# A two-block network on one core: the column halves of block two's norms cross the stage borders separately

## What is computed

```python
def rms_norm(x, g):
    xf = x.astype(jnp.float32)
    y = xf * lax.rsqrt(jnp.mean(xf * xf, axis=-1, keepdims=True) + EPS)
    return (y * g.astype(jnp.float32)).astype(x.dtype)

def ada_norm(h, g, shift, scale):
    return rms_norm(h, g) * (1 + scale) + shift

def second_block(...):
    h, hc = x, ctx
    for l in range(DEPTH):
        ...
        h = h + HALF * gt1 * swiglu(ada_norm(h, g_ffn1[l], sh1, sc1), w1_ffn1[l], w3_ffn1[l], w2_ffn1[l])
        hc = hc + HALF * cgt1 * swiglu(ada_norm(hc, g_ffn1[l], csh1, csc1), w1_ffn1[l], w3_ffn1[l], w2_ffn1[l])

        u = ada_norm(h, g_mix[l], sh2, sc2)
        uc = ada_norm(hc, g_mix[l], csh2, csc2)
        z_conv, z_cq, z_ckv, z_kr, z_four = split_mixing(u @ w_in[l])
        zc_conv, zc_cq, zc_ckv, zc_kr, zc_four = split_mixing(uc @ w_in[l])
        ...
        h = h + gt2 * y
        if not last:
            ...
            hc = hc + cgt2 * yc

        h = h + HALF * gt3 * swiglu(ada_norm(h, g_ffn2[l], sh3, sc3), w1_ffn2[l], w3_ffn2[l], w2_ffn2[l])
        if not last:
            hc = hc + HALF * cgt3 * swiglu(ada_norm(hc, g_ffn2[l], csh3, csc3), ...)
    return rms_norm(h, g_final)
```

## Time and profile before

| | us |
|---|---|
| median of 3 runs | 2830.51 |
| lowest, highest | 2826.48, 2833.05 |
| the profiled execution | 2829.12 |
| its span, first to last instruction | 2827.3 |
| busy in the span: PE / DVE / ACT / POOL | 2741.4 / 1776.6 / 1065.5 / 192.0 |

### The profile page before, as it was taken

How to read it: one execution, slowest core, us unless ns; L and a number is a source line. 1 busy time by engine, 2 the same in 40 slices (tenths; PEclk the granted TensorE clock), 3 DMA queues, 4 the chain that set the end, 5 groups by cost and what they waited for, 6 DMA issues and landing times.

```text
span 2827.3 us, 45215 instructions
## 1 busy us (share of the span) xinstructions
PE 2741.4 (97%) x16508; PEld 2334.7 (83%) x16508; DVE 1776.6 (63%) x3023; ACT 1065.5 (38%) x1704; POOL 192.0 (7%) x184
## 2 busy tenths in 40 slices
PE   8999999999999999999999999999999999899998
PEld 8669999589988888775777788888788888689998
DVE  7466656566676565587675665555665557756665
ACT  5356444366342221325434322222322214554443
POOL 0000000000000000032213000000000000134000
PEclk9999999999999999999999999999999999999999
DMA  5535544635544433321432244433344433244554
GB/s 194 197 117 196 183 165 156 216 131 184 180 142 141 148 139 132 115 72 64 137 133 66 90 142 148 141 135 131 130 142 148 142 126 120 83 129 156 168 177 157
DMA packets 118649, 401.16 MB, mean 142 GB/s; under 512 B 12928, under 2 KB 20992, under 8 KB 118144
## 3 DMA queue, kind: packets, MB, share of 16 engines
q1 hardware_dynamic: 115408, 392.48, 41.0%
q10 hardware_dynamic: 3120, 7.07, 0.7%
HBM read 398.45 MB, written 1.05 MB: 141 GB/s over the span
## 4 chain that ended last, share of the span: by engine, by line
PE 86%; DVE 5%; issue 4%; DMA 2%; ACT 1%; POOL 1%; DVEq 1%; ACTq 0%; POOLq 0%; SPq 0%
PE bank L836 24%; PE bank L843 24%; PE bank L840 24%; PE bank L1595 2%; DMA ring<-weights 1%; PE bank L2088 1%; PE bank L2447 1%; PE bank L2444 1%; PE bank L2441 1%; DVE work L2209 1%; DVE hn_lo L1069 1%; PE bank L934 1%; DVE w_lo L797 1%; POOL w_lo L797 1%; PE bank L1326 1%
## 5 line engine op out<-in xcount | busy, mean ns | idle before, releaser
L773 ACT ACTIVATE w_hi<-ring 128x1024 fp32r<-128x1024 f32 (+1 forms) x548 | 572.1, 1045 | 1158.3 <-DMA ring<-weights 1157.7
L797 DVE TENSOR_TENSOR w_lo<-ring,w_hi 128x1024 fp32r<-128x1024 f32 (+1 forms) x538 | 658.9, 1226 | 526.6 <-ACT w_hi L773 522.1
L840 PE MATMUL bank<-hn_hi,w_hi 128*128 128x256 f32 (+1 forms) x2848 | 896.9, 333 | 0.0
L843 PE MATMUL bank<-hn_lo,w_hi 128*128 128x256 f32 (+1 forms) x2848 | 896.7, 333 | 0.0
L840 PEld LDWEIGHTS bank<-hn_hi,w_hi 128*128 128x128 f32 x2848 | 542.2, 190 | 52.2
L843 PEld LDWEIGHTS bank<-hn_lo,w_hi 128*128 128x128 f32 x2848 | 542.2, 190 | 52.1
L836 PE MATMUL bank<-hn_hi,w_lo 128*128 128x256 f32 (+1 forms) x2848 | 570.4, 336 | 10.3 <-DVE w_lo L797 7.3
L836 PEld LDWEIGHTS bank<-hn_hi,w_lo 128*128 128x128 f32 x2848 | 453.7, 190 | 71.3 <-issue 11.5
L840 PE MATMUL bank<-hid_hi,w_hi 128*128 128x512 f32 (+1 forms) x704 | 248.7, 362 | 0.0
L843 PE MATMUL bank<-hid_lo_a,w_hi 128*128 128x512 f32 (+1 forms) x640 | 226.2, 362 | 0.0
L964 DVE SCALAR_TENSOR_TENSOR conds<-ring,con 128x1024 f32<-128x1024 f32 x106 | 131.3, 1239 | 58.8 <-DMA ring<-weights 42.0
(11 more groups left out here) (350 smaller groups left out, 3127.7 us busy)
## 6 DMA issues: line engine op xcount, KB each, us to landing
ring<-weights SPq DMA_DIRECT2D x694, 512.0 KB, 3.3
ring<-weights SPq DMA_DIRECT2D x32, 384.0 KB, 3.0
ring<-weights SPq DMA_DIRECT2D x32, 256.0 KB, 2.9
ring<-weights SPq DMA_DIRECT2D x28, 192.0 KB, 2.3
con<-consts ACTq DMA_DIRECT2D x1, 2063.0 KB, 9.5
con<-consts ACTq DMA_DIRECT2D x1, 1088.0 KB, 5.4
res<-ctx_cm ACTq DMA_DIRECT2D x1, 1024.0 KB, 7.7
con<-params ACTq DMA_DIRECT2D x1, 1024.0 KB, 11.0
```

The costliest lines, as they stand in the source:

```text
L773: act.activation(w_hi[:, slot, 0:w], ring[slot][:, 0:w], ACT.Copy).then_inc(s.w_hi, 1)
L797: eng.tensor_tensor(w_lo[slot][:, 0:w], ring[slot][:, 0:w], w_hi[:, slot, 0:w].bitcast(F32), ALU.subtract).then_inc(s.w_lo, 1)
L840: pe.matmul(dst, high, x_hi(k), start=False, stop=False)
L843: return pe.matmul(dst, high, x_lo(k), start=False, stop=(stop and k == order[-1]))
```

## The change

Norms 5 to 8 are done in halves from end to end. In the last group of the product before, PE finishes half 0 ahead of half 1 (`hidden_by_halves`, `mixed_by_halves`), DVE evicts it and PE takes its mean inside the product of half 1. DVE forms seven values of half 0, evicts half 1 (`evict_half`), and goes on with half 0, then half 1. The first pair of the next stage (`pair_by_halves`) does half 0 and then half 1, with the second mean after the sixth row. Norm 4's context half is computed during the down-projection: its squares by POOL, rstd before the first group, values, high and low parts two rows per group; the pair begins with it. The third weight split of five stages goes from DVE to POOL, its high part on ACT moves behind the last rstd. The values of norm 6 get a place of their own, so that they do not overwrite the merged branches that PE still reads. The groups concerned are written out one by one instead of as a loop on PE.

```diff
+THIRD_BY_POOL = (("ffn1", 0), ("conv_in", 0), ("ffn2", 0), ("ffn1", 1), ("conv_in", 1))
+MEAN_BEHIND = 5
+VALUES_EARLY = 7
...
+            if lin.third_by_pool and isinstance(number, int) and number == lin.split0 + 2 and not third:
+                return
...
+            if lin.third_by_pool and isinstance(number, int):
+                if number == lin.split0 + 2 and not third:
+                    return
+                if number in (lin.split0 + 2, lin.split0 + 3):
+                    eng.wait_ge(s.w_lo, number)
...
+        def is_halved(n):
+            return 2 * DEPTH < n < LAST_NORM - 1
+        def parts(n):
+            return 2 if is_halved(n) else 1
...
-                if before is not None:
+                if before is not None and not is_halved(n):
                     wait_last(act, before)
-            for c in range(w // T):
-                t = slice(c * T, (c + 1) * T)
-                act.wait_ge(s.mean_sq, streams_before(n) + c + 1)
-                act.activation(lnb[:, t], mean_bank(c), ACT.Ln, bias=eps_col)
-                act.drain()
-                act.activation(rstd[:, t], lnb[:, t], ACT.Exp, scale=-0.5).then_inc(s.rstd, 1)
             if n < 2 * DEPTH:
+                rstd_act(act, n, 0)
                 for k in range(KT):
                     act.wait_ge(s.norm_value, values_before(n) + k + 1)
                     act.activation(hn_hi[:, k, 0:w], sq[:, k, 0:w], ACT.Copy).then_inc(s.norm_hi, 1)
-            elif is_split(n):
-                l, which = divmod(n - 2 * DEPTH, 3)
-                for k in range(KT):
-                    act.wait_ge(s.norm_value, values_before(n) + k + 1)
-                    for c in range(w // T):
-                        t = slice(c * T, (c + 1) * T)
-                        last = act.activation(hn_hi[:, k, t], sq[:, k, t], ACT.Identity,
-                                              bias=modulation(l)[:, SHIFT[which], k, c:c + 1])
-                    last.then_inc(s.norm_hi, 1)
+                return
+            for c in range(parts(n)):
+                rstd_act(act, n, c)
+                if lin is not None and lin.third_by_pool and c == parts(n) - 1:
+                    split_high(act, lin, Group(0, 0, 0, period(lin.cpg)), 2, third=True)
+                if is_split(n):
+                    for k in range(KT):
+                        shifted_high(act, n, c, k)
...
+        def context_rstd(act):
+            wait_last(act, PLAN["up", DEPTH - 1])
+            act.wait_ge(s.ctx_ms, 1)
+            act.activation(rstd[:, T:2 * T], mean_bank(1), ACT.Ln, bias=eps_col)
+            act.drain()
+            act.activation(rstd[:, T:2 * T], rstd[:, T:2 * T], ACT.Exp, scale=-0.5).then_inc(s.ctx_rs, 1)
...
+        def norm_mean(pe, n, c):
+            t = slice(c * T, (c + 1) * T)
             pe.wait_ge(s.squares, squares_before(n) + KT - 1)
-            for c in range(w // T):
-                pe.matmul(mean_bank(c), ones_d, sumsq[:, c * T:(c + 1) * T], start=True, stop=False)
-            for c in range(w // T):
-                pe.wait_ge(s.squares, squares_before(n) + KT + c)
-                pe.matmul(mean_bank(c), ones_d, pr_b[:, c * T:(c + 1) * T], start=False, stop=True).then_inc(s.mean_sq, 1)
-        def norm_low(dve, n, k):
-            w = norm_width(n)
-            dve.wait_ge(s.norm_hi, KT * n + k + 1)
+            pe.matmul(mean_bank(c), ones_d, sumsq[:, t], start=True, stop=False)
+            pe.wait_ge(s.squares, squares_before(n) + KT + c)
+            pe.matmul(mean_bank(c), ones_d, pr_b[:, t], start=False, stop=True).then_inc(s.mean_sq, 1)
...
+        def pair_by_halves(pe, lin, n, w):
+            g = Group(0, 0, 0, period(lin.cpg))
+            dst = [bank[2 * parity(lin, g) + j] for j in range(2)]
+            wait_banks(pe, lin, g)
+            slot = [slot_of(lin, g, j) for j in range(2)]
+            for j in range(2):
+                pe.wait_ge(s.w_lo, lin.split0 + j + 1)
+            context_first = n == 2 * DEPTH
+            order = (1, 0) if context_first else (0, 1)[0:w // T]
+            for i, c in enumerate(order):
+                t = slice(c * T, (c + 1) * T)
+                for k in range(KT):
+                    if context_first and c:
+                        pe.wait_ge(s.ctx_hi, k + 1)
+                    else:
+                        pe.wait_ge(s.norm_hi, rows_before(n) + KT * c + k + 1)
+                    for j in range(2):
+                        pe.matmul(dst[j][:, t], w_lo[slot[j]][:, k * P:(k + 1) * P], hn_hi[:, k, t],
+                                  start=(k == 0), stop=False)
+                        pe.matmul(dst[j][:, t], w_hi[:, slot[j], k * P:(k + 1) * P], hn_hi[:, k, t],
+                                  start=False, stop=False)
+                    if i == 0 and k == MEAN_BEHIND:
+                        norm_mean(pe, n, 0 if context_first else 1)
+                for k in range(KT):
+                    if context_first and c:
+                        pe.wait_ge(s.ctx_lo, k + 1)
+                    else:
+                        pe.wait_ge(s.split_normed, rows_before(n) + KT * c + k + 1)
+                    for j in range(2):
+                        mm = pe.matmul(dst[j][:, t], w_hi[:, slot[j], k * P:(k + 1) * P], hn_lo[:, k, t],
+                                       start=False, stop=(k == KT - 1))
+                        if k == KT - 1 and c == order[-1]:
+                            mm.then_inc(used[slot[j]], 1)
+        def half_product(pe, lin, g, c, dst, x_hi, x_lo, start, stop, mean=None):
+            wait_split(pe, lin, g, c)
+            slot, rows = slot_of(lin, g, c), lin.tiles[c]
+            for k in range(rows):
+                pe.matmul(dst, w_lo[slot][:, k * P:(k + 1) * P], x_hi(k), start=(start and k == 0), stop=False)
+            for k in range(rows):
+                high = w_hi[:, slot, k * P:(k + 1) * P]
+                pe.matmul(dst, high, x_hi(k), start=False, stop=False)
+                mm = pe.matmul(dst, high, x_lo(k), start=False, stop=(stop and k == rows - 1))
+                if mean is not None and k == 1:
+                    norm_mean(pe, mean, 0)
+            return mm
...
+        def hidden_by_halves(pe, lin, g, n):
+            for half, c in [(0, 0), (1, 0)] + [(h, c) for h in range(2) for c in range(1, lin.own)]:
+                t, row = slice(half * T, (half + 1) * T), 8 * c
+                mm = half_product(pe, lin, g, c, bank[2 * parity(lin, g) + half][:, t],
+                                  lambda k: hid_hi[:, row + k, t], lambda k: hid_low(row + k)[:, t],
+                                  c == 0, c == lin.own - 1, n if half and c == 1 else None)
+                if half:
+                    mm.then_inc(used[slot_of(lin, g, c)], 1)
+                elif c == lin.own - 1:
+                    mm.then_inc(s.half_out, 1)
...
+        def mixed_by_halves(pe, lin, g, n):
+            for half in range(2):
+                t = slice(half * T, (half + 1) * T)
+                mm = half_product(pe, lin, g, 0, bank[2 * parity(lin, g) + half][:, t], lambda k: mrg_hi[:, k, t], lambda k: mrg_lo[:, k, t],
+                                  True, True, n if half else None)
+                mm.then_inc(used[slot_of(lin, g, 0)] if half else s.half_out, 1)
...
+                pe.wait_ge(s.ctx_sq, 1)
+                pe.matmul(mean_bank(1), ones_d, ctx_sum, start=True, stop=True).then_inc(s.ctx_ms, 1)
...
+                context_rstd(act)
+                for g in whole_groups(lin):
+                    splits_ahead(split_high, act, lin, g, after_down(l))
+                    for k in range(2 * g.m, min(2 * g.m + 2, KT)):
+                        context_high(act, k)
+                return
...
+                if context:
+                    for k in range(2 * g.m, min(2 * g.m + 2, KT)):
+                        context_value(dve, k)
+                    for k in range(max(2 * g.m - 2, 0), min(2 * g.m, KT)):
+                        context_low(dve, k)
...
-                if context and not is_last(g):
-                    square(dve, g.m, T, 2 * T)
                 dve.drain()
                 if is_last(g):
-                    for c in range(2 if context else 1):
-                        square_last(dve, c)
+                    square_last(dve, 0)
...
+        def context_squares(pool):
+            pool.wait_ge(s.ctx_in, 16)
+            pool.wait_ge(s.squares, squares_before(2 * DEPTH - 1) + KT)
+            for k in range(KT):
+                row = res[:, k, T:2 * T]
+                last = pool.tensor_tensor(ctx_tmp if k else ctx_sum, row, row, ALU.mult)
+                pool.drain()
+                if k:
+                    last = pool.tensor_tensor(ctx_sum, ctx_sum, ctx_tmp, ALU.add)
+                    pool.drain()
+            last.then_inc(s.ctx_sq, 1)
...
+            dve.wait_ge(s.rstd, streams_before(n) + 1)
+            if not is_halved(n):
+                for k in range(KT):
```

(49 more changed lines are left out.)

122 lines of the change are left out of this document (96 added, 26 removed).

## The result

The changed kernel takes 2847.68 us in the median of 6 runs (2841.08 to 2850.96), the kernel before 2831.10 in the median of 6; the ratio is 1.0058 (95%: 1.0042 to 1.0073). It is slower, by some 16 us instead of the forecast 6.9. The profiled execution took 2849.56 us with a span of 2847.8.

A forecast was written before the change was run, and what follows sets the result against it. TensorE, busy 97% of the span, was taken as the bound, so only its waits could shrink. Terms 3.2 + 3.2 + 0 - 2.2 - 2.2 + 0.4 + 1.2 + 3.3 = +6.9 us gave 2837.4 us; 8-in-10 range 2824 to 2845.

The forecast's parts named there:

- the 0.7 for the clock at norm 4: Border into ffn1, layer 0: PE's lower clock level after a gap of 2.8 us was taken to cost 0.7 us.
- V at norms 5, 7 and 8: Time of the next norm's first value, behind a 22-row product: 2.55 us later, as ACT waits for chunk 1's weight transfer.
- The halved norm, V + 16.0: Border's end after the first value: 12.7 us DVE operations, 0.9 eviction, 2.1 POOL block, 0.3 tail.
- The block by POOL's split, 2.1 us: In each of five borders, POOL's third weight split holds up DVE's values by 2.1 us, bounds 0 and 2.4.
- Norm 6, -1.5: Border into ffn2, layer 0, behind mix_out: end 2.2 us earlier; -1.5 with the clock and slot-release terms.
- Norm 4, -0.7 with all its terms: Border into ffn1, layer 0: -2.2 border, +0.4 early mean, +0.7 clock, +0.4 behind it.
- Norm 8, 0 and 1.1 for the clock: Border into conv_in, layer 1: DVE's split lets PE start the second group's second chunk as before, 0; clock 1.1 us.
- Slot release: Behind the first pair in ffn1 and ffn2, a weight slot freed later stalls PE 0.4 us, three times, +1.2.
- (a): Rival: POOL's split blocks nothing, each border 2.1 us shorter less 0.5 of PE's work; 2829.4 us, chance 0.25.
- (b): Rival, faster: (a), plus ACT not held at norms 5, 7, 8 and the clock high at all five; 2823 us, chance 0.12.
- (c): Rival: the clock costs more, low level for 5 to 6 us in three borders, +5; 2842.5 us, chance 0.13.
- (d): Case at norms 5, 7, 8: halves do not cross separately, since ACT's queue holds the first; part of the forecast.

The follow-up runs named there:

- experiment 4: Changed kernel with the last ffn1_out and ffn2_out groups doing chunk 1, both halves, before chunk 2; 2831.91 us, ratio 1.0010.
- experiment 7: Changed kernel, norms 5 to 8: ACT's Ln, Exp and seven high parts before chunk 1's split, DVE's eight values before its low split; 2851.57 us, ratio 1.0074.
- experiment 2: Kernel before with only norm 4's part of the change, norms 5 to 8 whole, POOL only norm 4's third split; 2835.34 us, ratio 1.0015.
- experiments 3: Changed kernel with all third splits back on DVE and ACT in their old places; 2839.57 us, ratio 1.0035.
- Experiment 8: Versions with mends together; the one with norm 8's third split between the halves on DVE, on the three-mends kernel: 2822.37 us, ratio 0.9968.
- experiment 6: Changed kernel with unread matmuls keeping TensorE busy in the gaps before the first pair at norms 4, 5, 7 and 8; 2845.94 us, ratio 1.0051.
- all mends together: Changed kernel: chunk 1 first, third splits of norms 4 to 8 on DVE (norm 8's between halves), norm 4's low split before the eviction; 2822.37 us, 0.9968.
- norms 4 and 6 alone: Halves at norm 6 only, norm 4's context part with low split before the eviction, no POOL third split, norms 5, 7, 8 as before; 2824.32 us, 0.9982.

## Why the prediction was wrong, point by point

The direction was right, and so was the late weight slot as its main cause; the size was off by more than the range allowed (2847.7 against 2845 at its upper end). The steps that failed are the 0 for norm 8 (1.1 with the clock, measured 3.7), the 0.7 for the clock at norm 4 (measured 1.8 in the mean), and the 0 for everything outside the five borders (norm 9 measured 2.1, the first 713 us 3.9). Point by point:

- **V at norms 5, 7 and 8** (2.55 us later, ACT held by the transfer): measured 20.89 - 18.11 = 2.8 at norm 5, and in the same way 2.5 at norm 7 and 3.1 at norm 8; experiment 4 takes it away. Right, and with it the sign named for it: ACT's split came 18.66 us after the group began instead of 14.45, with Ln directly behind it. But the held Ln is only one thing that the late slot does. In experiment 7 the first value comes 6.5 us sooner with the slot as late, and the border ends only 1.7 sooner, since PE's first matmul waits for the same chunk.
- **The halved norm, V + 16.0 and 0.6 for the clock:** V + 17.2 at norm 5. The clock cost 0.9 as DVE's idle time instead of 0.6 (0.3 and 0.7 in the other two traces, so right in the mean); 0.3 more went to DVE's own operations and the tail. Norm 5: 3.8 forecast, 4.1 measured. Norm 7: 4.2 and 5.3; there DVE's idle time was 0.3, 1.4 and 1.4.
- **The block by POOL's split, 2.1 us:** one value took 2622 ns at norm 5 where the others take 477; 2.14 more. Right at norms 4, 5, 7 and 8. At norm 6 the block went the other way, which the forecast did not have: DVE's values lost nothing, POOL's split took 8.66 us and PE waited 1.69 for it.
- **Norm 6, -1.5:** -1.7. The forecast's V is 1.9 us earlier, the measured one 2.1 (1627.34 against 1616.25 + 13.2). That the end fits too is in part luck: a block of 2.1 was expected and a wait of 1.69 took its place.
- **Norm 4, -0.7 with all its terms:** +1.1 in the mean. The step that failed is the clock term, 0.7. PE stood still for the 2.87 us that the forecast had as "gap 2.8", and in the first trace all 24 matmuls ahead of the mean ran at the lower of its two levels. The row of the first matmul, then windows of the changed kernel (length, busy us per engine, granted clock, DMA) at norm 4 and behind norm 8:

```profile
811.80 0.56 PE L1631 MATMUL bank<-hn_hi,w_lo 128*128 128x256 f32 x1 [2.87 <-DVE w_lo L822]
...
811.80:817.00 5.20, 5.20 (x24) 5.20 (x25) 0.00 (x0) 0.00 (x0) 0.00 (x0) 0.50 0.00 1
...
2387.20:2391.30 4.10, 4.10 (x22) 4.10 (x23) 1.03 (x1) 0.00 (x0) 0.00 (x0) 0.58 0.21 80
```

  24 matmuls in 5.26 us against 2.9: 2.4 us, on the path, since half 0's mean stands behind them. In the other two traces the same 24 took 4.45 and 4.43 and in experiment 2 4.30; in experiments 3, 4 and 7, behind the same gap of 2.87 us, 2.94 or 2.95. So the term is anything from 0 to 2.4, 1.8 in the mean of the three traces. With the slot release (below: 1.0, 1.3 and 1.0 instead of 0.4) this makes up the whole difference of 1.8 at this border.
- **Norm 8, 0 and 1.1 for the clock:** +3.7. This is the largest error of a border. The step that failed is that PE stands where it stood before, since DVE's queue lets the fourth chunk through at the same time. Rows of the changed kernel:

```profile
2380.66 1.70 PE L861 MATMUL bank<-hn_hi,w_lo 128*128 128x256 f32 x8 [1.81 <-POOL w_lo L822]
...
2387.15 1.50 PE L861 MATMUL bank<-hn_hi,w_lo 128*128 128x256 f32 x8 [1.90 <-DVE w_lo L822]
```

  With the 15.8 us by which the kernel was late there, the second should stand at 2385.8; it is 1.4 later. V is 0.55 of it, DVE's 32 operations with an idle time of 0.34 are 0.4, and two small operations that stand between them and the split, which the forecast left out, are 0.4. Then the matmuls behind it run at a granted clock of 0.58 for 4.1 us (the second window above), and 24 of them take 4.47 us (2387.15 to 2391.62) instead of 2.9: 1.6 more. The two parts make 3.0 of the first trace's 3.3; the forecast had 1.1 for the clock at this border in all, and 0 for the rest. Experiment 8 shows what the waits depend on: with DVE's third split between the halves the border is 2.1 us shorter than with POOL's.
- **Slot release, 0.4 at norms 4, 6 and 7:** In the first trace PE waits 1.03 at norm 4, nothing at norm 6 and 0.67 at norm 7 for the second group's second chunk, 1.7 in all against 1.2.
- **Nothing at norm 9, and nothing before 713 us:** 2.1 and 3.9 in the traces. The forecast had no step for either. Neither is in changed code. Norm 9's loss is 2.0 to 2.6 us in four of the kernels of the experiments, 1.3 in one and 0.2 to 0.7 in seven with the same operations there; what sets it is open. Of the first stretch, 14 traces of kernels with any part of the change are 2.3 us later on average than the mean of before's three, and the one of the written-out loops, whose time equals before's, is 3.0 later. How much of it is real is open.
- **The range.** With all of the clock's bound (7 instead of 3.3) the sum would have been 10.6, and the upper end of 14.5 above the median had 4 us in hand for everything else. Norms 7 and 8 and the two stretches without a step used more than that. The range had no term for stretches that are not changed.
- **Rivals.** (a), that POOL's split blocks nothing, is refuted by the 2622 ns; (b) falls with it. (c), that the clock pays more, was right in kind: some 1.1 us more at norm 4 and 0.5 at norm 8, not its +5, and the 2 us that experiment 6 got back are not clear of the noise. (d) was part of the forecast and held.

The page "SBUF — State Buffer" of the Trainium skill ("Who interferes with whom") has the block as an exclusive lock on ports that the two engines share, and says that the order of issue decides who blocks. The traces agree that one of the two engines stands still, with 2.1 us for a split of 2.47. They show besides how long POOL may stand: not for one of DVE's instructions but for all of its stream (below).

## What to carry to other kernels

Halving the work at a border pays only if the last thing that the next stage waits for comes earlier: here that was a weight slot, not the half norm, and a reordering of the last group's chunks gave back 13.6 us of 16. Even with all mends together the kernel gained 0.3% (0.9968), of which norms 4 and 6 alone give 0.2%. Before moving a border, write down for each of the next four waits what is queued in front of it on each engine; one split put behind eight values cost 4 to 6 us per border. And when an operation is moved to another engine to relieve the first, price the block between the two: 2.1 us beside the 1.2 us of DVE's split that was moved away. And where a term comes out of a sum as 0, list the operations that make it so: at norm 8 two small ones were left out.

## What the hardware showed unexpectedly

- **POOL's split and DVE's stream exclude each other in two ways.** Of 37 such splits beside a norm in nine traces, 24 took 2.42 to 2.53 us and DVE lost 2.1; 13 took 8.64 to 8.66 and DVE lost nothing until its 16 operations were through, after which its next one was lengthened by 2.0 to 2.2 us. There was no third kind. In all 24 DVE had been idle (0.32 us or more) just before its values; in all 13 it had come to them from the low parts without a gap. The two kinds in the changed kernel, norm 6 and norm 7:

```profile
1634.56 8.66 POOL L822 TENSOR_TENSOR w_lo<-ring,w_hi 128x1024 fp32r<-128x1024 f32 x1 [62.59 <-ACT w_hi L793]
2006.03 2.47 POOL L822 TENSOR_TENSOR w_lo<-ring,w_hi 128x1024 fp32r<-128x1024 f32 x1 [362.81 <-ACT w_hi L793]
```

  Whether the idle time decides or only goes with what does was not tried.
- **What the clock costs behind a gap differs between executions.** Behind one and the same gap of 2.87 us at norm 4, 24 matmuls took 2.94 or 2.95 (three kernels), 4.30 (experiment 2), 4.43 and 4.45 (two traces of the changed kernel) and 5.26 us (its first). The Trainium skill (TensorE: Matmul & The Clock Gate, Part 1) says that the number of slow matmuls at a kernel's start varies between runs of one kernel. These traces show the like behind a wait in mid-kernel, with the numbers just given; none of them bears on the start.
- **Written-out loops cost nothing that can be measured here:** 1.0004 (0.9995 to 1.0013).
